# The first twenty-five microseconds and one stage head of a four-layer kernel, put in another order

## The reference, cut to what matters

```python
def first_block(x, mix_norm, ...):
    for layer in range(DEPTH):
        h = rmsnorm(x, mix_norm[layer])
        ...
# even layer of second_block: u is the normed input, 16 heads of 128, 8 of kind a, 8 of kind b
u = rms_norm(h, ln_even_g[i])
proj = jnp.einsum('bsd,de->bse', u, w_in_even[i])
qa, ka, va, qb, kb, vb, gate = jnp.split(proj, even_splits, axis=-1)
qa = apply_axial_rope(rms_norm(qa.reshape(b, s, A_HEADS, HEAD_DIM_2), a_q_norm_g[i]), rope_tables)
ka = apply_axial_rope(rms_norm(ka.reshape(b, s, A_KV_HEADS, HEAD_DIM_2), a_k_norm_g[i]), rope_tables)
ya = gqa_attention(qa, ka, va)          # 8 heads, 2 heads of keys and values
yb = diff_attention(..., lam, slopes_b) # lam from exp of two dot products
yb = rms_norm(yb, b_subln_g[i], SUBLN_EPS) * (1.0 - lambda_init)
y = jnp.concatenate([ya, yb], axis=-1) * jax.nn.silu(gate)
h = h + jnp.einsum('bse,ed->bsd', y, w_out_even[i])
```

## Time and profile before

| | |
|---|---|
| median of 3 runs | 3174.37 us (3174.23 to 3177.27) |
| the profiled execution, its own time | 3170.98 us |
| its span | 3169.2 us, mean granted clock 0.996 |
| PE busy | 3121.3 us, 98% |
| DVE busy | 2317.2 us, 73% |
| ACT busy | 1649.6 us, 52% |
| start of unit 0's matmuls | 16.76 us |
| start of the even head (unit gates+0) | 2215.21 us |
| start of the even_a units | 2293.03 us |

### The profile page before, as it was taken

The page is one execution under the profiler, slowest core; times in us unless marked ns, Lnnn a source line. Parts: engine busy times, 40 slices in busy tenths (PEclk is TensorE's granted clock), DMA queues, the critical chain, the costliest instruction groups (busy, mean ns, idle before and its releaser), DMA issues.

```text
span 3169.2 us, 52302 instructions
## 1 busy us (share of the span) xinstructions
PE 3121.3 (98%) x18922; PEld 2775.8 (88%) x18922; DVE 2317.2 (73%) x3613; ACT 1649.6 (52%) x2203; POOL 13.5 (0%) x20
## 2 busy tenths in 40 slices
PE   8999999999999999999999999999899999999998
PEld 7988888888888899888888888888798888888887
DVE  6877886687677777888867876778676677666665
ACT  5664554454455467755544544554445654444443
POOL 1000000000000000000000000000000000000000
PEclk9999999999999999999999999999999999999999
DMA  5335555555555545555555555556434455444443
GB/s 203 130 126 193 186 185 199 177 192 191 183 187 190 200 159 177 176 199 186 185 200 180 191 197 175 190 191 213 147 120 160 160 173 178 169 170 172 172 170 135
DMA packets 81487, 561.56 MB, mean 177 GB/s; under 512 B 9552, under 2 KB 10576, under 8 KB 14288
## 3 DMA queue, kind: packets, MB, share of 16 engines
q1 hardware_dynamic: 81360, 559.87, 50.7%
HBM read 557.73 MB, written 2.10 MB: 177 GB/s over the span
## 4 chain that ended last, share of the span: by engine, by line
PE 85%; DMA 5%; DVE 5%; ACT 4%; issue 1%; SPq 0%; DVEq 0%; ACTq 0%
PE unit L313 49%; PE unit L316 26%; DVE w_tail L1345 2%; DMA raw<-in_lru_y 2%; ACT w_head L897 2%; DMA raw<-in_even_b 2%; PE unit L528 1%; PE unit L530 1%; PE unit L529 1%; PE o L402 1%; PE unit L697 0%; PE s L382 0%; PE s L465 0%; PE unit L699 0%; ACT pr L1242 0%
## 5 line engine op out<-in xcount | busy, mean ns | idle before, releaser
L1345 DVE TENSOR_TENSOR w_tail<-raw,w_head 128x2048 fp32r<-128x2048 f32 (+1 forms) x540 | 1208.7, 2239 | 143.6 <-ACT w_head L897 140.5
L897 ACT ACTIVATE w_head<-raw 128x2048 fp32r<-128x2048 f32 (+1 forms) x540 | 1013.0, 1876 | 500.8 <-DMA raw<-in_up 139.8
L313 PE MATMUL unit<-h,w_head 128*128 128x512 f32 x4912 | 1199.9, 392 | 0.0
L313 PEld LDWEIGHTS unit<-h,w_head 128*128 128x128 f32 x4912 | 902.1, 188 | 174.9
L316 PE MATMUL unit<-h,w_tail 128*128 128x256 f32 x4912 | 668.1, 285 | 0.0
L316 PEld LDWEIGHTS unit<-h,w_tail 128*128 128x128 f32 x4912 | 636.3, 192 | 21.6 <-issue 2.7
L313 PE MATMUL unit<-act,w_head 128*128 128x512 f32 x2384 | 580.3, 391 | 4.7 <-DVE prod L1354 4.7
L313 PEld LDWEIGHTS unit<-act,w_head 128*128 128x128 f32 x2384 | 438.4, 188 | 92.0 <-issue 5.8
L1354 DVE TENSOR_TENSOR prod<-unit,lo 128x256 f32<-128x256 f32 x465 | 196.5, 423 | 411.8 <-ACT lo L904 410.0
L904 ACT ACTIVATE lo<-unit 128x256 f32<-128x256 f32 x465 | 178.0, 383 | 611.1 <-PE unit L316 596.8
L316 PE MATMUL unit<-act,w_tail 128*128 128x256 f32 x2384 | 323.8, 283 | 0.0
(11 more groups left out here) (295 smaller groups left out, 2592.4 us busy)
## 6 DMA issues: line engine op xcount, KB each, us to landing
raw<-in_up SPq DMA_DIRECT2D x192, 1024.0 KB, 4.8
raw<-in_down SPq DMA_DIRECT2D x96, 1024.0 KB, 4.8
raw<-in_odd SPq DMA_DIRECT2D x64, 1024.0 KB, 4.8
raw<-in_even_b SPq DMA_DIRECT2D x32, 1024.0 KB, 4.8
raw<-in_attn SPq DMA_DIRECT2D x24, 1024.0 KB, 4.8
raw<-in_wo SPq DMA_DIRECT2D x16, 1024.0 KB, 4.9
raw<-in_lru_x SPq DMA_DIRECT2D x16, 1024.0 KB, 4.8
raw<-in_lru_y SPq DMA_DIRECT2D x16, 1024.0 KB, 5.2
```

The costliest lines, as they stand in the source:

```text
L313: pe.matmul(bank[:, :], w_head[:, slot, k * P:(k + 1) * P], src[:, k, :], start=k == 0, stop=False)
L897: a.activation(w_head[:, slot, 0:width], raw[:, r, 0:width], ACT.Copy).then_inc(head_done, 1)
L1345: v.tensor_tensor(w_tail[:, slot, 0:width], raw[:, slot % 2, 0:width], w_head[:, slot, 0:width].bitcast(F32), ALU.subtract).then_inc(tail_ ...
```

## The change

Three things are edited, and the program's results are the same.

1. The even head. `PHASES` has even_kv ahead of gates, so the four key and value units run first. The key norms are taken one unit later (in the middles of even_kv+2 and +3), the rotations in the middles of gate units 0 and 2, the transposes of the values in the middles of gate units 4 and 5. ACT and DVE get matching lists. The sums and the exponentials for `lam` and the scaled tables move from ahead of the stage to gate units 1 to 3. The six DMAs of the even tables are issued ahead of up10 in place of ahead of this stage.
2. The opening. SP issues the first weight block right behind `gains`, and `ones` behind the second quarter of `x`. ACT splits it and DVE makes its tail ahead of all `h` tiles. POOL squares tiles 0 to 7 and ACT tiles 8 to 15. PE takes four sums ahead of unit 0 and twelve within it. The parameters are made behind the second `tail`, the softplus chain in key unit 4, and `lo_half` of unit 0 stands ahead of the token norm.
3. even_b: `b_turn_p(i - 1)` moves from `early` to `middle` of unit 0, for i = 1 to 7.

```diff
-          + [("gates", 8), ("even_kv", 4), ("even_a", 8), ...
+          + [("even_kv", 4), ("gates", 8), ("even_a", 8), ...
+SQ_FIRST, SUMS_FIRST = 8, 4
...
             sp.dma_start(gains[:], t["gains"]).then_inc(cst_gain, 16)
+            sp.dma_start(raw[:, 0, :], t["attn"][0]).then_inc(loaded[0], 16)
             for c in range(4):
                 sp.dma_start(x[:, 4 * c:4 * c + 4, :], ...).then_inc(x_in[c], 16)
-                if c == 0:
-                    sp.dma_start(ones[:], t["ones"]).then_inc(cst_gain, 16)
-                    sp.dma_start(raw[:, 0, :], t["attn"][0]).then_inc(loaded[0], 16)
+                if c == 1:
+                    sp.dma_start(ones[:], t["ones"]).then_inc(ones_in, 16)
...
             for name, _ in PHASES:
-                if name == "gates":
+                if name == "up10":
                     sp.wait_ge(even_free, 1)
...
             def first_sum(k):
-                pe.wait_ge(sq_first, k + 1)
+                if k < SQ_FIRST:
+                    pe.wait_ge(sq_first, k + 1)
+                else:
+                    pe.wait_ge(sq_last, k - SQ_FIRST + 1)
...
-                for k in range(KT // 2):
+                for k in range(SUMS_FIRST):
                     first_sum(k)
...
-                    if k >= KT // 2:
+                    if k >= SUMS_FIRST:
                         first_sum(k)
...
-            for j in range(UNITS["gates"]):
-                unit(BASE["gates"] + j, j % RING, h, ready=... if j == 0 else None, norm=4 if j == 0 else None)
...
-            unit(b, b % RING, h)
-            unit(b + 1, (b + 1) % RING, h, (lambda: head_norm(nk, ones),))
-            unit(b + 2, (b + 2) % RING, h, (lambda: head_norm(nk + 1, ones, (rot_in, 1)), lambda: rotate(0, kv[:, 0, :])))
-            unit(b + 3, (b + 3) % RING, h, (lambda: rotate(1, kv[:, 1, :]),))
+            unit(b, 0, h, ready=(h_done, KT * 5), norm=4)
+            unit(b + 1, 1, h)
+            unit(b + 2, 2, h, (lambda: head_norm(nk, ones),))
+            unit(b + 3, 3, h, (lambda: head_norm(nk + 1, ones, (rot_in, 1)),))
+            unit(g, 0, h, (lambda: rotate(0, kv[:, 0, :]),))
+            unit(g + 1, 1, h)
+            unit(g + 2, 2, h, (lambda: rotate(1, kv[:, 1, :]),))
+            unit(g + 3, 3, h)
+            unit(g + 4, 0, h, (lambda: turn_v(vk, kv[:, 5, :], QS["even_a"]),))
+            unit(g + 5, 1, h, (lambda: turn_v(vk + 1, kv[:, 6, :], QS["even_a"]),))
+            unit(g + 6, 2, h)
+            unit(g + 7, 3, h)
...
-                    if n == 0 and k in (6, 10):
-                        turn_v(vk + k // 10, kv[:, 5 + k // 10, :], QS["even_a"])
...
-                b_unit(i, 0, (lambda: b_turn_p(i - 1),))
+                b_unit(i, 0, middle=(lambda: b_turn_p(i - 1),))
...
         def _(g):
-            for c in range(4):
+            for c in range(SQ_FIRST // 4):
...
+            split(0, 0)
+            a.wait_ge(cst_gain, 16)
...
-                if c == 1:
-                    split(0, 0)
             split(1, 1)
+            for m in range(SQ_FIRST, KT):
+                a.activation(store[:, m, :], x[:, m, :], ACT.Square).then_inc(sq_last, 1)
             split(2, 2)
+            lo_half(BASE["attn"], 0)
...
+            b, nk, vk = BASE["even_kv"], NORMS["even_kv"], VTS["even_kv"]
+            lo_half(b, 0)
+            head_square(nk, kv[:, 0, :])
+            step(b + 1, 1)
+            split(b + 2 + LEAD, 2 + LEAD)
+            head_root(nk, HD2)
+            head_square(nk + 1, kv[:, 1, :])
+            lo_half(b + 2, 2)
+            split(b + 3 + LEAD, 3 + LEAD)
+            head_root(nk + 1, HD2, used=(rot_in, 1))
+            lo_half(b + 3, 3)
...
             for j in range(UNITS["gates"]):
-                step(BASE["gates"] + j, j, j == 0)
+                split(BASE["gates"] + j + LEAD, j + LEAD)
+                if 4 <= j <= 5:
+                    copy_vt(vk + j - 4, kv[:, 1 + j, :])
+                lo_half(BASE["gates"] + j, j)
                 a.wait_ge(gate_in, j + 1)
                 a.activation(store[:, S_Q + j % 2, :], a_gate[j], ACT.Tanh, scale=0.5).then_inc(gate_th, 1)
...
+            tail(0, 0)
+            v.wait_ge(cst_gain, 16)
...
-                if c == 1:
-                    tail(0, 0)
             tail(1, 1)
             tail(2, 2)
...
             for j in range(RING):
+                if j == 2:
+                    head_scaled(nk, kv[:, 0, :], C_AK)
...
+            head_scaled(nk + 1, kv[:, 1, :], C_AK)
+            v.wait_ge(vt_in, VTS["even_kv"] + 2)
+            for j in range(UNITS["gates"]):
+                product(BASE["gates"] + j, j)
+                scaled(a_gate[j]).then_inc(gate_in, 1)
+                tail(BASE["gates"] + j + LEAD, j + LEAD)
+                v.wait_ge(gate_th, j + 1)
+                link(v.scalar_tensor_tensor(a_gate[j], ...))
+                if j in (0, 2):
+                    rope(j // 2, kv[:, j // 2, :], BASE["gates"] + j)
+                if j == 1:
+                    lambda_sums()
+                if j == 3:
+                    query_tables()
```

More of the change, by code:

```diff
@@ L970, in _ @@
                         .then_inc(h_head, 1)
-                if c == 1:
-                    split(0, 0)
             split(1, 1)
+            for m in range(SQ_FIRST, KT):
+                a.activation(store[:, m, :], x[:, m, :], ACT.Square).then_inc(sq_last, 1)
             split(2, 2)
+            lo_half(BASE["attn"], 0)
             a.wait_ge(eps_set, 1)
             token_norm(0)
[L977 to L980, removed]
             for g in range(KV_UNITS):
-                step(BASE["attn"] + g, g % RING)
+                if g:
+                    step(BASE["attn"] + g, g % RING)
+                else:
+                    split(BASE["attn"] + LEAD, LEAD)
                 if g < RING:
@@ L986, in _ @@
                     head_root(g, HD)
+                    if g == 0:
+                        a.wait_ge(par_in, 1)
+                        chain.link(a.activation(spl[:, 3, :], spl[:, 2, :], ACT.Exp, scale=-1.0))
+                        chain.link(a.activation(spl[:, 4, :], spl[:, 3, :], ACT.Identity, bias=1.0))
+                        a.activation(spl[:, 5, :], spl[:, 4, :], ACT.Ln).then_inc(par_done, 1)
                 else:
@@ L1181, in _ @@
             ffn(1, 3)
-            stage_split("gates")
-            a.wait_ge(lam_in, 1)
-            a.activation(lamb[:, 2:4], lamb[:, 0:2], ACT.Exp).then_inc(lam_done, 1)
+            stage_split("even_kv")
             token_norm(4)
+            b, nk, vk = BASE["even_kv"], NORMS["even_kv"], VTS["even_kv"]
[9 more added lines that the diff above has]
+            lo_half(b + 3, 3)
             for j in range(UNITS["gates"]):
-                step(BASE["gates"] + j, j, j == 0)
+                split(BASE["gates"] + j + LEAD, j + LEAD)
+                if 4 <= j <= 5:
+                    copy_vt(vk + j - 4, kv[:, 1 + j, :])
+                lo_half(BASE["gates"] + j, j)
                 a.wait_ge(gate_in, j + 1)
                 a.activation(store[:, S_Q + j % 2, :], a_gate[j], ACT.Tanh, scale=0.5).then_inc(gate_th, 1)
-            b = BASE["even_kv"]
-            nk, vk = NORMS["even_kv"], VTS["even_kv"]
+                if j == 2:
+                    a.wait_ge(lam_in, 1)
+                    a.activation(lamb[:, 2:4], lamb[:, 0:2], ACT.Exp).then_inc(lam_done, 1)
             a.preload_act_table_set(LN_EXP)
[L1196 to L1201, removed]
             def a_square(n):
@@ L1460, in _ @@
[L1460 to L1466, removed]
@@ L1483, in _ @@
             for g in range(KV_UNITS):
                 u = BASE["attn"] + g
+                if g == 0:
+                    parameters()
                 product(u, g % RING)
+                if g == 0:
+                    token_norm(0)
                 if g >= RING:
@@ L1488, in _ @@
                     tail(u + LEAD, g + LEAD)
+                    if g == RING:
+                        softplus()
                     continue
@@ L1741, in _, with lambda_sums, query_tables @@
             ffn(1, 3)
[L1744 to L1755, removed]
+            def lambda_sums():
+                for n in range(2):
+                    part = prod[:, 64 * n:64 * (n + 1)]
+                    link(v.tensor_tensor(part, kv[:, 7, 128 * n:128 * n + 64],
+                                         kv[:, 7, 128 * n + 64:128 * n + 128], ALU.mult))
+                    last = v.tensor_reduce(lamb[:, n:n + 1], part, AX.X, ALU.add)
+                last.then_inc(lam_in, 1)
+                v.wait_ge(lam_in, 1)
+            def query_tables():
+                v.wait_ge(lam_done, 1)
+                link(v.tensor_tensor(lamb[:, 4:5], lamb[:, 3:4], lamb[:, 2:3], ALU.subtract))
+                link(v.tensor_scalar(lamb[:, 5:6], lamb[:, 4:5], -LAMBDA_INIT, None, ALU.add))
+                v.tensor_scalar(store[:, S_COSQ, :], store[:, S_COS, :], dims[:, C_AQ:C_AQ + 1], None, ALU.mult)
```

(10 more changed lines are left out.)

66 lines of the change are left out of this document (33 added, 33 removed).

## The result

The changed kernel took 3153.52 us (median of 4 runs, 3151.19 to 3157.61), against 3174.3 us before (4 runs, 3172.89 to 3177.27): a ratio of 0.994, 95% interval 0.9927 to 0.9952. The profiled execution took 3151.62 us with a span of 3149.8 us; before it was 3170.98 us, so the two traces stand 19.4 us apart.

What follows compares the result with a forecast made beforehand. PE's own work, plus its waits and half-clock stretches, was taken to bound the kernel. Gains of 11.4 (even head), 3.0 (opening) and 0.2 (even_b) summed to 14.6 us, giving 3159.8 us from 3174.37 us; range 3154 to 3166 us.

Steps and rivals of the forecast that it cites:

- The even head: Key, value and gate units before even_a: PE never waits, 69.4 us to the first even_a unit; 11.4 us gained, bounds 8 to 12.
- the rival of late splits in ACT's list: Even head: ACT's new list makes splits late, two or three PE stalls, say 7 us, 3166.8 us; chance 0.10.
- The tables' DMAs: Even tables loaded ahead of up10: moving them gains 0, at most 1 us lost where 0.96 MB delay one block.
- The opening: Start of the kernel through unit 1: earlier block 0 and reordered work gain 3.0 us, bounds -1 to 6 us.
- The block was taken to land at 7.3 us: Opening: block 0, loaded second, lands once 1.7 MB has moved, 0.6 MB of it later DMAs, at about 7.3 us.
- the prediction's 6.2 us by this rule: Opening: with no share of later DMAs beside it, block 0 would land at about 6.2 us and the opening gain 5.0 us.
- The wait of 2.1 us in unit 1: Opening: PE's head norm waits 2.1 us for an ACT square behind block 3's split, where 2.3 us stood before.
- The half-clock stretch in unit 1: Opening, after PE's wait: 3.9 us gained without it, 1.9 us lost if it comes again; the middle, 3.0 us, was taken.
- even_b: Stage even_b: moving the transposes shifts PE's wait from L393 to L745; 0.2 us gained once, bounds 0 and 4.6 us.
- The rival that takes the list of waits at its word: even_b: PE's wait simply goes, 4.4 us more gained, 3155.4 us; chance 0.07.
- a ring without it: even_b: ACT, DVE and DMA wait for each other in 26.17 us without PE, which needs some 25.6 us and waits.
- The carry-over to the median: Whole run: the profiled execution's 3.4 us under the median is carried over, so 3156.4 us becomes 3159.8 us.

Runs made afterwards that it cites:

- old_dma_order: The changed kernel with SP's old order of the first DMAs (a quarter of x and `ones` ahead of the first weight block): 3152.52 us.
- pool_squares16: The changed kernel with all 16 squares left on POOL: 3155.92 us.

## Why the prediction was right or wrong

- **The even head, 11.4 us forecast, 11.6 us measured.** The count held: 69.4 us to the first even_a unit were forecast and 69.44 us measured. PE never waits, and the clock is 1.00. The second even_a unit follows after 5.8 us. So the rival of late splits in ACT's list is refuted.
- **The tables' DMAs, 0 forecast.** Ahead of up10 SP issues them from 1377.47 us, and the next load goes out at 1382.25 us. From the same matmul of lru_out (at 1377.22 us here, at 1384.69 us before) to the even head both traces take 830.51 us. That is right.
- **The opening, 3.0 us forecast, 6.2 us measured.** This is the term that failed, by its size and not by its sign, and it lies just beyond its own upper bound of 6 us. It has three parts:
  - The block was taken to land at 7.3 us, with 0.6 MB of later DMAs beside it; it landed by 6.17 us. Unit 0 ended at 24.59 us in place of 25.4 us: 0.8 us. By the window up to the landing (shown with old_dma_order) 1.41 MB had moved, of which the gains and the block are 1.1 MB. So 0.3 MB of later DMAs had gone beside it and not 0.6 MB, and more had moved by 6.17 us than before (199 GB/s, 1.23 MB). The step that failed is the one that carried the 0.6 MB over from a single landing, of a block that was the fourth DMA there (the prediction calls it the third). The Trainium skill, "DMA: Bandwidth & Descriptors", section "Two DMAs through the same engine are not ordered", has descriptors of one queue on an engine start in order; the prediction's 6.2 us by this rule is the time measured, though some later bytes did move before the block was complete.
  - The wait of 2.1 us in unit 1 is 0.1 us. DVE ended h at 19.45 us and not at 21.6 us: 1.3 us because its tail of block 0 ended at 10.62 us and not at 11.9 us, which is the landing once more, and 0.8 us because the sixteen tails of h took 8.91 us and not 9.7 us, with POOL's squares done at 15.6 us and not at 17.4 us. The tail of block 1 was earlier by as much, and so were the load and the split of block 3. Unit 1 took 6.55 us, where 33.5 - 25.4 = 8.1 us were forecast: 1.6 us.
  - The half-clock stretch in unit 1 did not come, nor the wait ahead of it. Of the two cases I had taken the middle: 0.9 us. By the window before, 3.47 us at 0.55, the stretch cost 1.6 us. Taking the middle was a guess, and the runs give no better one: a wait of 2.33 us was followed by 0.55, one of 3.58 us in pool_squares16 by 1.00.
- **even_b, 0.2 us forecast, 0.3 us measured.** The wait moved to the turn of the output, as forecast, and the head went from 26.39 to 26.30 us (26.15 to 26.30 us in the kernels with the moved transposes and the old root, 26.34 to 26.39 us in the others). The rival that takes the list of waits at its word is refuted. But the reason was half of the truth: I had PE only as a follower of a ring without it. There were two rings of nearly the same length, and the second runs through PE.
- **The carry-over to the median.** The profiled execution before lay 3.4 us under its median, the one after 1.9 us: 1.5 us. Another 1.2 us came between unit 2 and the even head, where nothing was edited; the forecast had no term for it.

Together: 3.3 us from the opening (3.24 before rounding), 0.2 from the even head, 0.1 from even_b, 1.2 and 1.5 from these two make the 6.3 us between 3159.8 and 3153.52 us. No rival came true. The total fell 0.5 us below the range because the errors of the opening, of the stretch where nothing was edited and of the carry-over all went one way.

## What to carry to other kernels

Where several engines wait for each other in a ring, removing PE's wait shows the next ring and not the gain. Follow the ring back through every engine and queue once, then once more with the first edge cut: in even_b two moves that are worth nothing or 1 us alone are worth 6 us together. In the list of an engine, try what frees others ahead of what waits for a load; here that paid only once the other ring was cut too. And count a stage on a saturated engine by its units: that gave the even head to 0.2 us, where the chain of landings, splits and tails of the opening was off by half.

## What the runs showed of the hardware

POOL and DVE slow each other. A square on POOL took 0.61 us while DVE stood, 0.79 us beside DVE's tails of h and 2.66 us for the one under DVE's tail of a block; a tail of h on DVE took 0.47 us alone and 0.83 us beside POOL (4, 8 and 16 squares on POOL give 7.13, 8.91 and 11.40 us for the sixteen tails). From 4 to 16 squares that is 4.27 us, so each square on POOL costs DVE about 0.36 us (0.45 us from 4 to 8, 0.31 us from 8 to 16). The Trainium skill, "SBUF — State Buffer", section "SBUF: two separate sides", has GpSimd and a VectorE instruction with two SBUF inputs take one pair of ports in turns, each for a whole instruction; the trace agrees, in that the square's 2.66 us are about the length of the tail that it ran into (2.50 to 2.72 us).

A stretch of the recurrence, with the same instructions, differed by up to 5 us over twelve traces (203.5 to 208.9 us). A change of 3 us in the opening is plain in the starts of matmuls (unit 2 at 34.1 to 34.2 us in place of 31.1 to 32.0 us), and medians of 4 and 5 runs do not separate it surely.
